# Three edits of one kernel: when a top-k search runs, how a differential head joins its maps, and which engine issues zero rows

## What is computed

```python
for l in range(2):
    h = rms_norm(x, attn_norm[l])
    fq,fk,fv,ff, dq,dk,dv, sq,sk,sv, iq,ik,iw = split(h @ w_in[l])
    # 6 heads: causal attention with a decay from log_sigmoid(ff)
    o_fox = fox_attention(norm(fq), norm(fk), fv, cumsum(log_sigmoid(ff + fb)))
    # 4 heads of two maps each: both are softmaxes over the keys, values are shared
    p = softmax(causal(q @ k))                  # two maps of each head
    o_diff = (p[:, :, 0] - lam * p[:, :, 1]) @ dv ; o_diff = rms_norm(o_diff) * (1 - lam_init)
    # 6 heads that see only the 128 best keys of an index score
    score = sum_h(iw_h * relu(iq_h @ ik)) ; sel = top_k(score, 128)
    o_dsa = attention over sel
    x = x + concat(o_fox, o_diff, o_dsa) @ w_out[l]
    x = x + (silu(gate) * up) @ w_down[l]
```

## Time and profile before

| | |
|---|---|
| time, median of 3 runs | 2157.55 us (2155.32 to 2158.45) |
| profiled execution | 2156.96 us, its span 2155.2 us |
| TensorE clock granted, mean | 0.954 |
| busy: PE, DVE, ACT, POOL | 1975.8 (92%), 1204.0 (56%), 850.7 (39%), 524.3 (24%) us |
| instructions: PE, DVE, ACT, POOL | 11384, 2338, 1402, 447 |

### The profile page before, as it was taken

The page is one execution under the profiler, slowest core; times in us unless marked ns, Lnnn a source line. Parts: engine busy times, 40 slices in busy tenths (PEclk is TensorE's granted clock), DMA queues, the critical chain, the costliest instruction groups (busy, mean ns, idle before and its releaser), DMA issues. The chain is left out here.

```text
span 2155.2 us, 30251 instructions
## 1 busy us (share of the span) xinstructions
PE 1975.8 (92%) x11384; PEld 1718.4 (80%) x11384; DVE 1204.0 (56%) x2338; ACT 850.7 (39%) x1402; POOL 524.3 (24%) x447
## 2 busy tenths in 40 slices
PE   6998898999999999889899999998998989799994
PEld 6898787888888889878788888878986878677773
DVE  3557875444543454787544453379922243488885
ACT  4354454222211344455421221133234452277772
POOL 2665421000000256533100000025543444200001
PEclk9999898999999999999999999999999999799997
DMA  4112322313221111232232322125657732689995
GB/s 163 60 60 68 85 84 115 126 63 117 102 73 59 53 68 43 79 94 67 108 131 83 117 82 93 59 100 108 108 138 233 206 127 108 230 326 410 409 410 199
DMA packets 73534, 288.80 MB, mean 134 GB/s; under 512 B 18241, under 2 KB 23105, under 8 KB 48961
## 3 DMA queue, kind: packets, MB, share of 16 engines
q1 hardware_dynamic: 64768, 255.67, 35.1%
q10 hardware_dynamic: 6048, 22.02, 2.6%
q0 software_dynamic: 2592, 9.44, 1.2%
HBM read 244.14 MB, written 37.19 MB: 131 GB/s over the span
## 5 line engine op out<-in xcount | busy, mean ns | idle before, releaser
L1295 PE MATMUL fill_ps<-w_hi,h_hi 128*128 128x256 f32 (+1 forms) x704 | 210.2, 299 | 7.9 <-PEq L3161 5.1
L1295 PE MATMUL fill_ps<-w_hi,h_lo 128*128 128x256 f32 (+1 forms) x704 | 205.3, 292 | 0.0
L1295 PE MATMUL fill_ps<-w_lo,h_hi 128*128 128x256 f32 (+1 forms) x704 | 205.0, 291 | 0.0
L322 POOL TENSOR_SCALAR norm_ss<-norm_ss 128x1 f32<-128x1 f32 x24 | 4.8, 201 | 796.3 <-ACT ffn_raw_d L316 739.0
L845 POOL TENSOR_TENSOR w_lo<-w_raw,w_hi 128x512 fp32r<-128x512 f32 x120 | 162.2, 1376 | 143.3 <-ACT w_hi L913 143.1
L516 DVE TENSOR_TENSOR ffn_silu<-ffn_silu,ffn_up 128x512 f32<-128x512 f32 x44 | 30.2, 687 | 286.6 <-ACT ffn_silu L474 286.6
L1792 POOL TENSOR_TENSOR w_lo<-w_raw,w_hi 128x512 fp32r<-128x512 f32 x96 | 144.7, 1535 | 137.6 <-ACT w_hi L1876 137.6
L474 ACT ACTIVATE ffn_silu<-ffn_up 128x512 f32<-128x512 f32 x44 | 26.3, 598 | 337.1 <-PE ffn_up L575 337.1
L528 DVE TENSOR_TENSOR x<-ffn_down,x 128x512 f32<-128x512 f32 x176 | 119.1, 689 | 71.2 <-PE ffn_down L590 70.4
L575 PE MATMUL ffn_up<-h_hi,w_hi 128*128 128x512 f32 x384 | 152.1, 396 | 3.5 <-PEq L792 3.5
L1295 PEld LDWEIGHTS fill_ps<-w_hi,h_hi 128*128 128x128 f32 x704 | 142.0, 202 | 13.1 <-issue 10.6
(11 more groups left out here) (454 smaller groups left out, 5352.3 us busy)
## 6 DMA issues: line engine op xcount, KB each, us to landing
moe_raw_gu<-in_w_e_gu SPq DMA_DIRECT2D x46, 1024.0 KB, 11.2
w_raw<-in_w_mix SPq DMA_DIRECT2D x28, 1024.0 KB, 5.0
w_raw<-in_w_two SPq DMA_DIRECT2D x23, 1024.0 KB, 5.2
moe_raw_d<-in_w_e_down SPq DMA_DIRECT2D x23, 1024.0 KB, 7.9
w_raw<-in_w_gate SPq DMA_DIRECT2D x22, 1024.0 KB, 5.6
w_raw<-in_w_up SPq DMA_DIRECT2D x22, 1024.0 KB, 6.7
ffn_raw_d<-in_w_down SPq DMA_DIRECT2D x22, 1024.0 KB, 4.9
moe_in<-in_zero SPq DMA_DIRECT2D x23, 512.0 KB, 8.0
```

Of the source, the lines that this page charges most:

```text
L322: self.core.nc.gpsimd.tensor_scalar(s_t, s_t, 1.0 / D, NORM_EPS, ALU.mult, ALU.add).then_inc(self.rooted, 1)
L1295: last = nc.tensor.matmul(b[:, 0:cols], aw[:, k, t * P:(t + 1) * P], ww[:, k, 0:cols], start=k == 0 and n == 0, stop=k == KD - 1 and n == 2)
```

## The change

The search: eight rounds stand ahead of the loop instead of three, the others are spread over fewer steps, and the index scores are computed earlier among the dense tiles. The normalisation of the third group comes after seven rounds. The differential heads: the exponents of the first map stay unturned in free space of the output tile; when the second map has its exponents, DVE scales and adds both (`combine`), and only the joined map is turned, multiplied by the values and stored. Some dense parts, units and a split stand at other steps. The second mixer: the zero rows are issued by ACT, one block a step from step 9, and the first stack copies wait for the matmuls of L2433 alone.

```diff
-TOP_EARLY = 3
+TOP_EARLY = 8
...
-    DENSE.setdefault(_n // 3 if _n < 36 else 12 + (_n - 36) * 11 // 12, []).append(_x)
-UNIT_AT = {4: 4, 5: 5, 8: 6, 9: 7, 12: 8, 13: 9, 16: 10, 17: 11, 18: 12, 20: 13, 26: 14, 28: 15, 44: 16, 45: 17, 51: 18, 56: 19}
+    DENSE.setdefault(_n // 3 if _n < 36 else 12 + (_n - 36) * 3 // 4 if _n < 48 else 22 + (_n - 48) * 11 // 12 if _n < 60 else _n - 27, []).append(_x)
+UNIT_AT = {4: 4, 5: 5, 8: 6, 9: 7, 12: 8, 13: 9, 16: 10, 17: 11, 19: 12, 21: 13, 26: 14, 28: 15, 44: 16, 45: 17, 51: 18, 56: 19}
...
-SPLIT_AT = {6: 0, 7: 4, 8: 8, 9: 19, 10: 25, 11: 36, 12: 45, 13: 60, 14: 72, MIX_CHUNKS: 83}
+SPLIT_AT = {6: 0, 7: 4, 8: 8, 9: 18, 10: 25, 11: 36, 12: 45, 13: 60, 14: 72, MIX_CHUNKS: 83}
...
-SEARCH_AT = {_n: _j for _j, _n in enumerate(_m for _m in range(44) if _m % TB < 2 or _m in (22, 26, 30, 34))}
+SEARCH_AT = {_n: _j for _j, _n in enumerate((0, 1, 5, 8, 17, 20, 21, 24, 25, 28, 29, 32, 33, 36, 40, 41))}
...
+FIRST_MAP = {a for a in range(DIF0, DSA0) if (a - DIF0) % 2 == 0}
+TURNED = [n for n in range(STEPS) if n // TB not in FIRST_MAP]
+RANK = {n: r for r, n in enumerate(TURNED)}
...
+        prob_first = [o[:, 2:3, D - P:D], o[:, 0:2, D - P:D], o[:, 0:3, D - 2 * P:D - P], o[:, 0:TB, D - 3 * P:D - 2 * P]]
...
-        order = [("dense", n) for n in range(3 * TB)] + [("idx", n) for n in range(3)]
-        order += [("dense", n) for n in range(3 * TB, 5 * TB - 1)] + [("unit", 0), ("unit", 1), ("dense", 5 * TB - 1), ("unit", 2), ("unit", 3)]
+        order = [("dense", n) for n in range(3 * TB - 2)] + [("idx", n) for n in range(3)]
+        order += [("dense", n) for n in range(3 * TB - 2, 5 * TB - 1)] + [("unit", 0), ("unit", 1), ("dense", 5 * TB - 1), ("unit", 2), ("unit", 3)]
...
+                    if a in FIRST_MAP:
+                        dst, scores = prob_first[i], s_ps[n % 3][:, 0:(i + 1) * P].rearrange("p (b n) -> p b n", n=P)
+                        if a > DIF0:
+                            act.wait_ge(combined, combines(n - TB))
+                    else:
+                        dst, scores = prob[i][:], s_ps[n % 3][:, 0:(i + 1) * P]
+                        if a:
+                            act.wait_ge(turned, max(RANK[m] for m in TURNED if m < n and m % TB == i) + 1)
+                    nc.scalar.activation(dst, scores, ACT.Exp, bias=neg_max[:, i:i + 1],
+                                         scale=-1.0, accum_out=row_sum[a % 4][:, i:i + 1]).then_inc(exped, 1)
...
+                def combine(n):
+                    a, i = divmod(n, TB)
+                    if i == 0:
+                        dve.wait_ge(exped, n)
+                        link(nc.vector.tensor_scalar(first_sum[:], row_sum[(a - 1) % 4][:], lam[:], None, ALU.mult))
+                    dve.wait_ge(exped, n + 1)
+                    link(nc.vector.reciprocal(share[:, i:i + 1], row_sum[a % 4][:, i:i + 1]))
+                    nc.vector.tensor_tensor(share[:, i:i + 1], share[:, i:i + 1], first_sum[:, i:i + 1], ALU.mult).then_inc(shared, 1)
+                    dve.wait_ge(shared, combines(n))
+                    second = prob[i][:].rearrange("p (b n) -> p b n", n=P)
+                    nc.vector.scalar_tensor_tensor(second, second, share[:, i:i + 1], prob_first[i], ALU.mult, ALU.add).then_inc(combined, 1)
...
+                weigh(1)
+                weigh(2)
                 sum_squares(1)
-                normalise(1, 0)
-
                 dve.wait_ge(ones, 3)
                 dve.wait_ge(c_sum, 1)
                 c_of = o_ps[:, 0:TB * FOX].rearrange("p (t h) -> p t h", t=TB).unsqueeze(3)
                 nc.vector.tensor_scalar(fqk[:, :, 0:FOX, HEAD:HEAD + 1], c_of, HEAD ** 0.5, None, ALU.mult).then_inc(c_done, 1)
                 nc.vector.tensor_scalar(fqk[:, :, FOX:2 * FOX, HEAD + 1:HEAD + 2], c_of, -HEAD ** 0.5, None, ALU.mult).then_inc(c_done, 1)
-                for i in BLK:
-                    weigh(i)
+                weigh(TB - 1)
+                normalise(1, 0)
                 dve.wait_ge(weighed, 3 * IDX)
                 for i in BLK:
                     diag = top[i][:, i * P:(i + 1) * P]
                     nc.vector.tensor_tensor(diag, diag, const[:, C_ROPE - P:C_ROPE], ALU.add).then_inc(masked, 1)
                 dve.wait_ge(masked, 3)
-                sum_squares(2)
                 for r in range(TOP_EARLY):
                     find(r)
                     take(r)
-                    if r == 0:
+                    if r == TOP_EARLY - 3:
+                        sum_squares(2)
+                    if r == TOP_EARLY - 2:
                         normalise(2, 0)
...
-                    if n >= 7 and n % TB == 3 and n < STEPS + 4:
+                    if n % TB == 3 and n - 4 in RANK:
                         store((n - 7) // TB)
                     if n < STEPS:
                         score_max(n)
-                    if 2 <= n < STEPS + 2 and (n - 2) % TB < 2:
+                    if n - 1 in RANK and DIF0 <= (n - 1) // TB < DSA0:
+                        combine(n - 1)
+                    if n - 2 in RANK and (n - 2) % TB < 2:
...
-                    if n in MIX_AT:
-                        m = MIX_AT.index(n)
-                        dve.wait_ge(stored, DIF0 + 4 * m + 4)
-                        for h in range(4 * m, 4 * m + 4, 2):
-                            nc.vector.scalar_tensor_tensor(od[:, :, h, :], od[:, :, h + 1, :], lam[:], od[:, :, h, :],
-                                                           ALU.mult, ALU.add).then_inc(mixed, 1)
...
+                    if n >= 3:
+                        pe.wait_ge(exped, n - 2)
...
+                    i, r = n % TB, RANK[n]
+                    if DIF0 <= n // TB < DSA0:
+                        pe.wait_ge(combined, combines(n))
+                    else:
+                        pe.wait_ge(exped, n + 1)
...
+                        if c == 2 and t == 2:
+                            pe.wait_ge(idx_ready, 1)
+                            for m in range(3):
+                                turn_idx(m)
                         for part in range(len(PARTS)):
                             dense(c, t, part)
+                        if c == 2 and t >= 2:
+                            if t == 2:
+                                pe.wait_ge(idx_out, 3)
+                            score_idx(t - 1)
...
-                pe.wait_ge(idx_ready, 1)
-                for m in range(3):
-                    turn_idx(m)
                 for t in range(TB):
                     for part in range(len(PARTS)):
                         dense(3, t, part)
-                    if t < TB - 1:
-                        if t == 0:
-                            pe.wait_ge(idx_out, 3)
-                        score_idx(t + 1)
+                    if t == 0:
+                        score_idx(TB - 1)
...
-                    if 2 <= n < STEPS + 2:
+                    if n - 2 in RANK:
...
+ZERO_AT = 9
...
-                        sp.wait_ge(y_summed, 1)
+                        sp.wait_ge(within_summed, 1)
...
-                    zero_rows(3 * j, 3 * j + 3)
...
+                    if 0 <= n - ZERO_AT < BLOCKS:
+                        b = n - ZERO_AT
+                        act.dma_start(core.moe_in[b * P:(b + 1) * P, :], w["zero"].partition_broadcast(P)).then_inc(emptied, 16)
...
-                        nc.tensor.matmul(y_of(g), within[:, g, :], u_c[:, g, :], start=g // 2 % 8 == 0, stop=False)
+                        last = nc.tensor.matmul(y_of(g), within[:, g, :], u_c[:, g, :], start=g // 2 % 8 == 0, stop=False)
+                    last.then_inc(within_summed, 1)
```

More of the change, by code:

```diff
@@ L697, in mixer @@
         spare = core.sb("mix_spare", [P, 8], ctx=st)
-        row_sum = [core.sb(f"row_sum{s}", [P, TB], ctx=st) for s in range(2)]
+        row_sum = [core.sb(f"mix_row_sum{s}", [P, TB], ctx=st) for s in range(4)]
         inv_sum = core.sb("inv_sum", [P, TB], ctx=st)
+        first_sum = core.sb("first_sum", [P, TB], ctx=st)
+        share = core.sb("map_share", [P, TB], ctx=st)
         prod = rope_a[:, 0:2 * DIFF_D].rearrange("p (m d) -> p m d", m=2)
@@ L769, in split, with copied, stores, combines @@
             return 2 * (c - 1) + h + 1
-        def dve_copies(n):
-            return sum(1 for m in range(n) if m % TB < 2)
+        def copied(n):
+            return (pt_dve if n % TB < 2 else pt_act), sum(1 for m in TURNED if m <= n and (m % TB < 2) == (n % TB < 2))
+        def stores(a):
+            return len([b for b in range(a) if b not in FIRST_MAP])
+        def combines(n):
+            return sum(1 for m in range(n + 1) if DIF0 <= m // TB < DSA0 and m in RANK)
         def group(p):
@@ L977, in exp @@
                     act.wait_ge(maxed, n + 1)
[L978 to L983, removed]
+                    if a >= 4:
+                        act.wait_ge(stored, stores(a - 3) + (a - 4 in FIRST_MAP))
+                    if a in FIRST_MAP:
[8 more added lines that the diff above has]
```

(20 more changed lines are left out.)

47 lines of the change are left out of this document (25 added, 22 removed).

## The result

The changed kernel takes 2181.28 us (median of 4 runs, 2175.32 to 2185.98) against 2158.0: a ratio of 1.011, 95% interval 1.0087 to 1.0133. The forecast was 2162 with a range up to 2180: the right side, but past the range.

A forecast was written before the change was run, and what follows sets the result against it. PE sets the pace first, and over the differential heads PE and DVE hold each other up. Per layer 11 + 2.5 - 5 = +8.5, twice +17; 2156.96 + 17 - 11.5 = 2162.5, said as 2162, range 2142 to 2180.

The forecast's parts named there:

- The search ahead of the loop: Ahead of step 0: six rounds before the third group's squares delay the first row maximum, +11 us a layer.
- my upper end: Ahead of the loop: the search term becomes +14 us a layer if the half clock stays.
- Rival B: Ahead of the loop: POOL's chain overlaps the search more, +6.6 in place of +11, total 2154; chance 0.11.
- Dense parts and units: Steps 12 to 23: moved dense parts and later units cost +2.5 us a layer, ends -3.4 and +6.
- The joined maps: Heads 6 to 13: PE loses 11.7 us of work, the bound passes to DVE; 77 us against 82, -5 a layer.
- the 82 that I had named as a sign of being wrong: Heads 6 to 13: the forecast is wrong if they take under 72 us or over 82.
- my two bounds: Heads 6 to 13: DVE's work needs 80.1 us at its present share, 72.6 at 0.96; middle taken as 77.
- A: Heads 6 to 13: DVE fills its gaps once PE has slack, 69.7 us (-12.3), total 2143; chance 0.20.
- C: Second mixer: only head 0 gains, weights and y stay in SP's queue ahead of head 2; 2171, chance 0.10.
- D: Heads 6 to 13: PE stands more and loses clock, 0.70, 85 us, +3 not -5; 2178, chance 0.07.
- E: Heads 6 to 13: joins beside POOL are slow, +4.2 us a layer, 2171; chance 0.12.
- The zero rows: Second mixer: zeros on ACT and earlier stack copies end waits for units of heads 0 and 2, -11.5 us.

The follow-up runs named there:

- e2: Kernel before with eight search rounds ahead of the loop, earlier index scores and the new half-round list alone: 2183.71 us, ratio 1.0124.
- e5: Changed kernel with all sixteen half rounds in steps 0 to 21, none in heads 6 to 13: 2178.76 us, ratio 1.0126.
- e9: Kernel before with zero rows on ACT, early half rounds, three rounds ahead of the loop, no join: 2144.13 us, ratio 0.9939.
- e11: Changed kernel with DVE's join left out, the first map's output part missing, the second map turned after its exponents: 2152.36 us, ratio 0.9976.
- e14: As e13, but with half rounds where the kernel before has them: 2155.11 us, ratio 0.9992.
- e13: Kernel before with zero rows on ACT, joined maps, early half rounds, three rounds ahead, joined maps alone turned a step later: 2147.36 us, ratio 0.9949.
- e10: Changed kernel with half rounds in steps 0 to 21 and transposes, copies, values, stores a step later for all heads: 2180.64 us, ratio 1.0100.

## Why the prediction was wrong, point by point

**The search ahead of the loop: mechanism right, size short.** I forecast +11 a layer from 11.7 of rows; it was 13.8 and 14.1, twice some 3 of the error. The chain behind the squares was as read. The 2.1 us that the sum missed are in front of the rounds: the squares begin at 102.87 and not at 100.7, as the three masks took 1.79 us where they had taken 0.69, and the last two products of the weighing 2.88 where three had taken 2.46. Both ran beside POOL's splits, which now lie there from 76.01 for 7.01 us. The weighing began 8.4 us earlier (7.9 forecast), so the half clock at dense(3,0), my upper end, was not the cause. PE stood for 15.8 us in front of unit 1, about 12 forecast. Rival B (the chain of POOL hides it) did not occur.

**Dense parts and units: too dear.** +0.5 and +1.0, forecast +2.5. The wait for the stack grew only to 3.2 (4 forecast), the one for POOL shrank to 2.9. I had also counted wrong: by the two lists of dense parts only one part more falls into steps 12 to 23 (15 against 14), not two.

**The joined maps: this step failed.** Its sentence was that "the bound passes to DVE, and PE's gain is worth only what DVE can take up", with -5; it was +2.5 and +4.4. The heads take 84.6 and 84.2 us, over the 82 that I had named as a sign of being wrong, and DVE is busy for 0.85 of them, not 0.90. (The middle of my two bounds, 80.1 and 72.6, is 76.4 and not 77, which is small beside this.)

The runs contradict the sentence: e2 took 5.6 us from DVE for next to nothing, and e5 took 13 from it and left the wait. What bounded these heads before was PE's own work. e9 and e11 leave DVE nearly the same to do (58.4 and 57.8 us) and differ in PE's work (72.3 and 62.3 us), and these heads take 80.6 and 72.6 us; e2, with 62.8 us on DVE and PE's work whole, takes 80.6 too.

What the change put in its place is a wait in PE's queue. DVE joins the map of a step only after the row maximum of the next step, and the join itself is three dependent operations; PE wants the joined map first thing in the step after. Between the score that this row maximum needs and the turn, PE has little to do: from 235.74 to 237.1 one score and one dense part, for instance, and then it stands until 239.31 (there a half round, too, stood in front of the row maximum). While it stands, the score and the dense part behind the turn wait too. I had seen this wait and called it covered by the dense parts of its step; one part stands in front of the turn and covers about 1.3 us, the next one is queued behind it. DVE's load does count once this wait is eased: e14 has 9.7 us more of it in these heads than e13 and takes 5.2 us longer there.

The account of the 84.6 us: PE has 7.6 us less of busy time and 10.1 more of standing. Of work it lost more. Busy time by mean clock, an estimate, is 72.9 x 0.90 = 65.6 before and 65.3 x 0.81 = 52.9 after, 12.7 less, near the 13.5 of the forecast, so some 5 us went to the lower clock.

**The rivals.** A (DVE fills its gaps) and C (only head 0 gains) did not occur. D (the clock) did in part: 0.81, not the 0.70 I priced. The price was wrong as well: I divided 59.3 us by 0.70 as if they had been taken at full clock, but the rows they come from have about 0.90, and 59.3 x 0.90 / 0.70 is 76 us, not 85. The clock does not follow the standing alone (0.86 in e5 with 20.0 us of it, 0.83 in e10 with 14.6), and no run held it fixed, so its share stays open, as do the 4.6 us between e10 and e11. E (joins slow beside POOL) is there in size: the joins take 0.35, 0.73, 0.86 and 1.05 us for the four widths against 0.34, 0.48, 0.62 and 0.75, 3 us a layer, and the products of one column 0.32 against 0.16, 2 us more. It is part of the wait, too. Inside the 18.0 us lie products of 1.10 and 0.42 us and joins of 1.45 and 1.59 that take 0.16, 0.16, 0.48 and 0.62 elsewhere: about 3 us, an estimate from these rows. No run had the joins without POOL beside them, so this share is not shown.

**The zero rows: right, a little small.** -14.0, forecast -11.5; both waits went. The Trainium skill, "DMA: Bandwidth & Descriptors", "Queues, rings and completion order", has each queue row take its turn on the same DMA engines; by that rule 6.6 was sure and the rest only in part. It did not decide here: in the changed kernel the units of head 2 land in time beside the zeros of ACT's queue. The gain is of two edits, the zeros and the earlier stack copies; no run parts them.

**The sum.** Forecast +17 - 11.5 = +5.5; measured in the profiles +34.9 - 14.0 = +20.9. Of the 15.4 between them the heads, with the wrong sign, are 16.9 (6.9 in two layers, -10 forecast) and the search 5.9 (27.9, 22 forecast); steps 0 to 3 took back 2.4, the dense steps 3.5, the second mixer 2.5, and what follows the heads added 1.1.

## What to carry to other kernels

Ask of an added wait not only how long the chain in front of it is, but what stands behind the waiting instruction in its own queue: work that could cover a wait covers nothing if it is queued after it. A busy share near 0.85 on two engines does not tell which of them to relieve; a run that takes work from one of them alone does. And of an edit of several parts, run each alone: here one part carried the gain and two the loss.

## What the runs showed of the hardware

Short DVE operations with two operands in SBUF got much longer beside POOL. The product of one column takes 0.16 us, but 1.10 at 219.33, when POOL's operation of 219.15 was running; both end at 220.4. The join of 256 columns takes 0.48, but 1.45 at 242.93 beside the splits from 239.39. The first POOL row stood beside the slow masks:

```profile
219.33 1.10 DVE L1187 TENSOR_TENSOR map_share<-map_share,first_sum 128x1 f32<-128x1 f32 x1
...
223.01 0.48 DVE L1190 SCALAR_TENSOR_TENSOR prob<-prob,map_share,mix_out 128x256 f32<-128x256 f32 x1
```

```profile
76.01 7.01 POOL L859 TENSOR_TENSOR w_lo<-w_raw,w_hi 128x512 fp32r<-128x512 f32 x4
...
219.15 1.26 POOL L883 TENSOR_TENSOR unit_lo<-unit_in,unit_hi 128x512 fp32r<-128x512 f32 x1
...
239.39 6.13 POOL L859 TENSOR_TENSOR w_lo<-w_raw,w_hi 128x512 fp32r<-128x512 f32 x4
```

The Trainium skill, "SBUF — State Buffer", "SBUF: two separate sides", says that of a DVE operation with two SBUF inputs and a GpSimd operation that reads SBUF, the one that starts first holds a shared port for its whole instruction, and the other waits. With that rule the product that ends with POOL's operation agrees.
